# Last stage of a two-block model kernel turned from features to tokens in the partitions

## The chip, the cores and the metric

The kernel runs as one program on one core of a Trainium2 chip. The metric is the device time of that program in microseconds (us); before the change it is 944.46 us, the median of three runs (943.92 to 945.84). The engines that matter are TensorE (PE, with its weight loads as PEld), VectorE (DVE), ScalarE (ACT) and SyncE (SP), which only issues transfers here.

## The reference

A first block (short convolution mixer, convolutional feed-forward, latent attention, feed-forward) feeds a second one (a gated linear attention mixer and a squared-ReLU MLP). The change concerns only the end of the second block, for 256 tokens of 1024 features:

```python
h_lat = h_lat + mod_l[5] * sqrelu_mlp(modulate(rmsnorm(h_lat, norm2_g[i]), mod_l[3], mod_l[4]),
                                      mlp_w1[i], mlp_w2[i])
...
return rmsnorm(h_lat, final_g)
```

`sqrelu_mlp` is relu(x @ w1)**2 @ w2, with w1 of 1024 x 4096 and w2 of 4096 x 1024. The last matrix product, the gated addition to `h_lat` (1024 gates `mod_l[5]`, one per feature) and the last row norm with its gains `final_g` are what is rewritten. Everything is float32.

## The kernel before

**Weights as a stream.** All weights come through SP from DRAM in units of 128 x 1024 numbers (512 KB), into a ring of four tiles `raw`. Of each unit ACT makes a rounded copy `whi` (`hi`, L1007) and DVE the rest `wlo` = `raw` - `whi` (`lo`, L1528). Activations are kept in the same two parts. A product takes three matmuls: high by high, low by high, high by low. The rings `whi` and `wlo` have four slots too, so `hi` of unit u waits until PE is done with unit u - 4, and SP loads unit u when DVE has finished `lo` of unit u - 4. `slots_done` counts finished `lo`, `pe_units` counts units that PE has used up.

**The last stage** (`mlp_down`, 32 units) has the features of the output in the partitions. `units` multiplies with a 128 x 128 block of weights as the stationary operand and the 256 tokens as the moving one. In the first 28 units the high and the low part of the activations pass in one matmul of 512 columns (L501, `both=m2`), and a second one of 256 columns takes the low weights (L502). In the last 4 units there are three matmuls of 256 columns (L498, L499, L502). Four units make one tile of 128 output features; eight tiles go in turn to the PSUM banks `ps[0]` and `ps[1]`. DVE adds each tile with its gate to `h` (L2251), ACT squares it (L1016), DVE adds up the squares (L1546).

**The end.** After the last tile: DVE adds it to `h` (L2251), ACT squares it (L1500), PE sums the squares over the partitions (`column_stat`, L564 and L567), ACT takes the root (L1028), DVE the reciprocal (L1560), PE spreads it over the partitions (`spread`, L575), DVE multiplies `h` in four parts (L2270), and SP stores the four parts (L421). The gains were put on `h` by ACT meanwhile (`gained`, L1489).

**Other names.** `moving` (L530 to L532) is a function already in the kernel, used for the value projections and for some keys: there activations are the stationary operand and 512 columns of weights move. `h` holds the residual stream. `x2` (with its halves `xhi`, `xlo`), `yhi`, `ylo`, `khi`, `klo`, `zhi`, `zlo` and `m2` (with `mhi`, `mlo`) hold activations of different stages. `side` and the `ada` tiles carry the weights of the gates, whose dot products DVE makes between other work; the last of them belong to `mlp_up`, the stage ahead of the last. `vt` is a table of per-feature vectors, loaded at the start.

All on-chip tiles lie one behind the other in each partition, in the order of their declaration (`sb`), and tiles of stages that exclude each other share space. Worked out from the declared sizes, `x2` starts 95,136 bytes into the partition, `yhi` and `ohi` and `m2` at 111,520, `khi` at 177,056, `zhi` at 208,896 and `zlo` at 217,088; `whi` and `wlo` start at 16,384 and 32,768.

The order of the work is written out by hand: each engine's program is a list, with semaphores between them. Most stages are unrolled; the first 24 units of the last stage are a loop of three.

Of the kernel before, what the change touches and what calls it, by code (L numbers as in the profile page):

```python
# [23 lines left out]
P = 128  # L24
T = 256
# [20 lines left out]
OUT_PARTS = ((0, 2), (2, 4), (4, 6), (6, 8))  # L46
# [52 lines left out]
for _name, _n in [("g_mix0", 8), ("g_ffn0", 8), ("g_kvin", 8), ("g_mix1", 8), ("g_q", 4), ("g_kv", 2),  # L99
                  ("g_ffn1", 8), ("g_fin1", 8), ("g_n1", 8), ("g_n2", 8), ("g_fin2", 8), ("g_head", 8),  # L100
# [77 lines left out]
def program(nc, stream, xT, ctxT, vec, cst, rot, wa2, crow, out):  # L178
# [5 lines left out]
    with ctx:  # L184
# [105 lines left out]
        stage = ExitStack()  # L290
        m2 = sb("m2", 2 * MC * T, F32R, stage)
# [5 lines left out]
        raw_bias = sb("raw_bias", 4, F32, stage)  # L297
        stage.close()
# [63 lines left out]
        def _(sp):  # L362
# [52 lines left out]
            with sp.Fori(0, POSITIONS // RING - done // RING) as g:  # L415
                load_group(g * RING + done, g * RING + done - RING)
            for p in range(POSITIONS // RING * RING, POSITIONS):
                load_next(p)
            for n, (first, last) in enumerate(OUT_PARTS):
                sp.wait_ge(ev("out_chunk"), n + 1)  # L420
                sp.dma_start(out[:, first * T:last * T], h[:, first * T:last * T]).then_inc(ev("stored"), 16)  # L421
            sp.wait_ge(ev("stored"), 16 * len(OUT_PARTS))

# [12 lines left out]
        def _(pe):  # L436
# [537 lines left out]
            c.take(y_ready, MC - LATE)  # L974
            c.n["y_ready"] += LATE
            looped(DC // 2 - 1, 8, MC, mhi, mlo, lag=2, final=c.n["y_ready"], both=m2)
            units(4, MC, mhi, mlo, lag=2, both=m2)
            units(4, MC, mhi, mlo, lag=2)
            column_stat("last_square")
            spread()  # L980

        @block.scalar
        def _(act):
# [504 lines left out]
            def gained(k):  # L1488
                act.activation(at(h, k), at(h, k), ACT.Copy, scale=col("g_fin2", k)).then_inc(ev("gained"), 1)  # L1489

            def mlp_down(first, last=False):
                for m in range(2):
                    hi(4)
                    if last and m == 1:
                        act.wait_ge(sq_ready, c.value(sq_ready))
                        for k in range(DC - 1):
                            gained(k)
# [9 lines left out]
            with c.loop(DC // 2 - 1, {hi_ready: 8, tile_read: 2, sq_ready: 2}) as i:  # L1507
                mlp_down(i * 2)
# [764 lines left out]
def columns(v, n):  # L2273

    return v.reshape(n, P).T
# [107 lines left out]
```

## Time and profile before

| | us |
|---|---|
| median of 3 runs | 944.46 |
| lowest and highest | 943.92, 945.84 |
| profiled execution, first to last instruction (its span) | 944.4 |
| of it PE busy | 933.6 |
| first matmul of the last stage starts at | 847.01 |
| its last product matmul ends at | 936.09 |
| first store of the result is issued at | 939.71 |

The profile page gives an execution as its span; there is 0.1 us between that and the median of the runs, so nothing else of size lies around it. In the rows further down, times are from the start of the span, "x48" counts instructions, and a duration of a matmul overlaps with the next one: what a matmul costs in a stream is the distance between two starts, called its pitch here.

### The profile page before, as it was taken

Reading aid. Unit: us, or ns where it says so; the run is one execution under the profiler, and the core shown is the slowest. Engines: PE = TensorE matmul, PEld = TensorE weight load, DVE = VectorE, ACT = ScalarE, POOL = GpSimd, SP = SyncE. Lnnn points to the kernel's source line nnn. Section 1 sums busy time; section 2 is a strip of 40 time slices with the busy share of each in tenths; the row PEclk is TensorE's granted clock in tenths of the full one; section 3 lists DMA queues with packets and bytes.
Section 4 is the critical chain, followed back from the end, with each engine's and each line's share of the span. In section 5 each row is a group of like instructions: output and inputs, shape, how many; then the busy total and the mean of one; then the engine's idle time right before and its main releaser. Section 6 shows DMA issues by size and latency. Waiting matters only on the chain.

```text
span 944.4 us, 19749 instructions
## 1 busy us (share of the span) xinstructions
PE 933.6 (99%) x6952; PEld 889.8 (94%) x6952; DVE 798.0 (85%) x1317; ACT 564.0 (60%) x934; POOL 1.8 (0%) x8
## 2 busy tenths in 40 slices
PE   9999999999999999999999999999999999999997
PEld 8999999999999999999999999988899988888886
DVE  6999899999989888899999987955868889886553
ACT  6645656666455665766666556977533668674342
POOL 0000000000000000000000000000000000000000
PEclk9999999999999999999999999999999999999998
DMA  8776575557776554565557765563674348776661
GB/s 296 245 268 229 184 273 193 195 181 277 250 269 208 174 180 157 179 199 179 183 192 269 250 241 180 175 225 134 222 252 173 112 158 265 234 236 223 180 199 44
DMA packets 53877, 195.49 MB, mean 207 GB/s; under 512 B 6110, under 2 KB 6366, under 8 KB 53696
## 3 DMA queue, kind: packets, MB, share of 16 engines
q1 hardware_dynamic: 53680, 193.72, 61.5%
q10 hardware_dynamic: 144, 1.05, 0.3%
q8 instruction: 35, 0.57, 0.2%
q14 instruction: 18, 0.15, 0.0%
HBM read 193.69 MB, written 1.05 MB: 206 GB/s over the span
## 4 chain that ended last, share of the span: by engine, by line
PE 94%; DVE 4%; ACT 1%; issue 1%; DVEq 0%; ACTq 0%
PE ps L502 25%; PE ps L498 20%; PE ps L499 19%; PE ps L501 10%; PE ps L530 2%; PE ps L532 2%; PE ps L531 2%; DVE wlo L1528 1%; PE ps L609 1%; PE ps L792 1%; PE ps L808 1%; PE ps L651 1%; PE ps L652 1%; PE ps L653 1%; PE ps L674 1%
## 5 line engine op out<-in xcount | busy, mean ns | idle before, releaser
L1528 DVE TENSOR_TENSOR wlo<-raw,whi 128x1024 fp32r<-128x1024 f32 x303 | 367.0, 1220 | 72.9 <-ACT whi L1007 71.8
L1007 ACT ACTIVATE whi<-raw 128x1024 fp32r<-128x1024 f32 x303 | 317.0, 1052 | 90.8 <-PE ps L502 58.9
L502 PE MATMUL ps<-x,wlo 128*128 128x256 f32 x1248 | 349.5, 280 | 0.0
L498 PE MATMUL ps<-x,whi 128*128 128x256 f32 x1024 | 289.1, 282 | 0.0
L499 PE MATMUL ps<-x,whi 128*128 128x256 f32 x1024 | 286.9, 280 | 0.0
L502 PEld LDWEIGHTS ps<-x,wlo 128*128 128x128 f32 x1248 | 234.9, 188 | 0.0
L498 PEld LDWEIGHTS ps<-x,whi 128*128 128x128 f32 x1024 | 192.8, 188 | 0.8 <-issue 0.2
L499 PEld LDWEIGHTS ps<-x,whi 128*128 128x128 f32 x1024 | 192.8, 188 | 0.6 <-issue 0.5
L502 PE MATMUL ps<-yhi,wlo 128*128 128x256 f32 x400 | 112.1, 280 | 0.0
L498 PE MATMUL ps<-yhi,whi 128*128 128x256 f32 x400 | 112.1, 280 | 0.0
L499 PE MATMUL ps<-ylo,whi 128*128 128x256 f32 x400 | 112.1, 280 | 0.0
L1053 ACT ACTIVATE cv<-U,vt 128x256 f32<-128x256 f32 x88 | 44.9, 511 | 85.4 <-DVE U L1672 85.4
L501 PE MATMUL ps<-x,whi 128*128 128x512 f32 x224 | 78.1, 393 | 1.0 <-DVE mr L2212 0.6
L501 PE MATMUL ps<-m,whi 128*128 128x512 f32 x224 | 77.7, 392 | 0.0
L498 PEld LDWEIGHTS ps<-yhi,whi 128*128 128x128 f32 x400 | 75.3, 188 | 0.0
L499 PEld LDWEIGHTS ps<-ylo,whi 128*128 128x128 f32 x400 | 75.3, 188 | 0.0
L502 PEld LDWEIGHTS ps<-yhi,wlo 128*128 128x128 f32 x400 | 75.3, 188 | 0.0
L502 PE MATMUL ps<-m,wlo 128*128 128x256 f32 x256 | 71.6, 280 | 0.0
L501 PEld LDWEIGHTS ps<-x,whi 128*128 128x128 f32 x224 | 42.0, 188 | 11.0 <-DVE wlo L1528 1.0
L501 PEld LDWEIGHTS ps<-m,whi 128*128 128x128 f32 x224 | 42.1, 188 | 9.3
L502 PEld LDWEIGHTS ps<-m,wlo 128*128 128x128 f32 x256 | 48.0, 188 | 0.0
L1570 DVE SCALAR_TENSOR_TENSOR cv<-U,vt,cv 128x256 f32<-128x256 f32 x96 | 45.9, 479 | 0.6 <-ACT cv L1153 0.6
(333 smaller groups left out, 1536.6 us busy)
## 6 DMA issues: line engine op xcount, KB each, us to landing
raw<-stream SPq DMA_DIRECT2D x343, 512.0 KB, 4.0
side<-stream SPq DMA_DIRECT2D x16, 512.0 KB, 4.7
h<-xT SPq DMA_DIRECT2D x2, 512.0 KB, 6.1
c<-ctxT ACTq DMA_DIRECT2D x1, 1024.0 KB, 6.2
out<-h SPq DMA_DIRECT2D x4, 256.0 KB, 2.4
ct<-cst SPq DMA_DIRECT2D x1, 898.5 KB
rt_tab<-rot SPq DMA_DIRECT2D x1, 704.0 KB
state<-crow SPq DMA_DIRECT2D x1, 512.0 KB, 6.5
```

The source lines that it names most:

```text
L498: pe.matmul(dst, whi[:, w], at(hi, k), start=(k == 0), stop=False)
L499: pe.matmul(dst, whi[:, w], at(lo, k), start=False, stop=False)
L501: pe.matmul(ps[t % lag][:, :], whi[:, w], halves_of(both, k), start=(k == 0), stop=False)
L502: last = pe.matmul(dst, wlo[:, w], at(hi, k), start=False, stop=(k == K - 1))
L530: pe.matmul(dst, hi[:, tok], whi[:, w], start=first, stop=False)
L531: pe.matmul(dst, lo[:, tok], whi[:, w], start=False, stop=False)
L532: last = pe.matmul(dst, hi[:, tok], wlo[:, w], start=False, stop=final)
L609: pe.matmul(ps[7][:, 0:T], U[:, 0:P], U[:, 0:T], start=True, stop=True)
L1007: c.sig(act.activation(whi[:, s * D:(s + 1) * D], raw[:, r * D:(r + 1) * D], ACT.Copy), hi_ready)
L1053: c.sig(act.activation(at(cv, j), U[:, j * (T + 2) + 2:(j + 1) * (T + 2)], ACT.Copy, scale=vt_col(i * 12 + (base + 3 * j + 2))), tap_ready)
L1528: c.sig(dve.tensor_tensor(wlo[:, w], raw[:, r], whi[:, w], ALU.subtract), slots_done)
L1570: c.sig(dve.scalar_tensor_tensor(out=at(cv, j), in0=U[:, o + 1:o + T + 1], scalar=w1, in1=at(cv, j), op0=ALU.mult, op1=ALU.add), seq_dve)
```

## The change

The last stage is turned around. The output now has tokens in the partitions: `ps[2 * n + tk]` collects token half `tk` (128 tokens) of the features n * 512 to n * 512 + 511. The stationary operand is a 128 x 128 piece of the activations, the moving one is 512 columns of weights. The columns of w2 are laid out on the host as `wide`, in two halves of 16 units each.

- Matmuls: 12 of 512 columns per unit instead of 8 of 512 and 8 of 256 (the same 6144 columns). The last 4 units are taken first for token half 0, then for token half 1.
- The residual `h` has to be turned. DVE transposes it in 32 x 32 blocks (`turned_h`, eight instructions) behind `lo` of units 5 to 12, and SP moves the blocks to their place in `h_rows` with 32 transfers of 32 partitions x 8 x 32 numbers, eight each behind the loads of units 17 to 20.
- The gates are needed as a row in every partition: SP writes `mod[:, 5 * DC:6 * DC]` to DRAM (`gate_out`, 1024 single numbers) behind the load of unit 6 and reads it back into 128 partitions behind that of unit 8. The gains of the last norm come as a row from DRAM (`gain_row`, 512 KB) during `mlp_up`.
- Per quarter of the output (`row_sum`): DVE multiplies the bank with the gates, adds to `h_rows`, multiplies with the gains; ACT squares with an accumulated sum. Two quarters follow unit 19 and 20, two are at the end. The row norm needs no PE: root on ACT, reciprocal on DVE, and each quarter is scaled by one factor per partition, the first half of the features by ACT, the second by DVE. The result is stored as rows, in four parts.
- The column `g_fin2` leaves `vt`, which is 8 columns shorter; `m_pad` of 8 columns is put ahead of `m2`. With the declared sizes every tile behind `vt` starts 32 bytes earlier (`x2` at 95,104, `zhi` at 208,864), except `m2` and those behind it, which stay.

The core of the diff:

```diff
+        sb("m_pad", 8, F32, stage)
         m2 = sb("m2", 2 * MC * T, F32R, stage)
...
+            for p in range(done, POSITIONS):
                 load_next(p)
...
+                if u == GATE_AT:
+                    sp.wait_ge(ev("gate_known"), 1)
+                    sp.dma_start(gate_out.rearrange("k p -> p k"), mod[:, 5 * DC:6 * DC], allow_slow_non_contiguous=True)\
+                        .then_inc(ev("gate_stored"), 16)
...
+                elif ROWS_AT <= u < ROWS_AT + 4:
+                    if u == ROWS_AT:
+                        sp.wait_ge(ev("h_turned"), DC)
+                    for j in range(8):
+                        row_block(u - ROWS_AT, j)
...
-            looped(DC // 2 - 1, 8, MC, mhi, mlo, lag=2, final=c.n["y_ready"], both=m2)
-            units(4, MC, mhi, mlo, lag=2, both=m2)
-            units(4, MC, mhi, mlo, lag=2)
-            column_stat("last_square")
-            spread()
+            def row_products(slot, u, tk):
+
+                n, pair = u // HALF_UNITS, u % HALF_UNITS
+                for b in range(2):
+                    k = 2 * pair + b
+                    w = slice(slot * D + b * W, slot * D + (b + 1) * W)
+                    tok = slice(k * T + tk * P, k * T + (tk + 1) * P)
+                    dst = ps[2 * n + tk][:, :]
+                    pe.matmul(dst, mhi[:, tok], whi[:, w], start=(k == 0), stop=False)
+                    pe.matmul(dst, mhi[:, tok], wlo[:, w], start=False, stop=False)
+                    last = pe.matmul(dst, mlo[:, tok], whi[:, w], start=False, stop=(k == MC - 1))
+                return last
...
+            for u in range(MC - SPLIT, MC):
+                late.append(slot_of_next_unit())
+                last = row_products(late[-1], u, 0)
+            last.then_inc(ev("rows_done"), 1)
+            for u in range(MC - SPLIT, MC):
+                last = row_products(late[u - MC + SPLIT], u, 1)
+            last.then_inc(ev("rows_done"), 1)
...
+                new, old = row_part(gained, n, tk), row_part(h_rows, n, tk)
+                dve.tensor_tensor(new, ps[i][:, :], gate_row[:, n * W:(n + 1) * W], ALU.mult).then_inc(ev("row_gated"), 1)
+                dve.wait_ge(ev("row_gated"), i + 1)
+                dve.tensor_tensor(old, old, new, ALU.add).then_inc(ev("rows_summed"), 1)
+                dve.wait_ge(ev("rows_summed"), i + 1)
+                dve.tensor_tensor(new, old, gain_row[:, n * W:(n + 1) * W], ALU.mult).then_inc(ev("rows_gained"), 1)
...
+            while c.n["unit"] < UNITS:
+                lo()
+                u = c.n["unit"] - 1 - PHASE_AT["mlp_down"]
+                if 0 <= u - TURNS_AT < DC:
+                    turn_h(u - TURNS_AT)
+                elif u in (HALF_UNITS + RING - 1, HALF_UNITS + RING):
+                    row_sum(0, u - HALF_UNITS - RING + 1)
+                elif u == HALF_UNITS + RING + 4:
+                    row_bias()
```

The end of PE's program before, where the last tile's products are followed by the sums over the partitions and the spreading (the names after "<-" are moving and stationary operand):

```order
L502 MATMUL ps1<-m2,wlo 128x256
L564 MATMUL ps4<-ct,ssum 128x1 [waits ssum_ready,root_ready]
L564 MATMUL ps4<-ct,ssum 128x1
L567 MATMUL ps4<-ct,sq 128x1 [waits last_square]
L567 MATMUL ps4<-ct,sq 128x1
L575 MATMUL ps4<-ct,spare 128x128 [waits rstd_ready]
```

Nothing of this follows the products any more. The first products of the last stage now, behind those of `mlp_up` in `ps3`:

```order
L549 MATMUL ps3<-x2,wlo 128x256
L1031 MATMUL ps0<-whi,m2 128x512 [waits y_ready,tile_read,slots_done]
L1032 MATMUL ps0<-wlo,m2 128x512
L1033 MATMUL ps0<-whi,m2 128x512
```

Operands have changed places and every matmul has 512 columns. SP's list in the last stage now, with the issues that stand between the loads (before there were only loads and the four stores):

```order
L400 DMA raw<-stream 128x1024 [waits slots_done] x9
L447 DMA h_rows<-turned_h 32x8x32 [waits h_turned]
L447 DMA h_rows<-turned_h 32x8x32 x7
L400 DMA raw<-stream 128x1024 [waits slots_done]
L447 DMA h_rows<-turned_h 32x8x32 x8
L400 DMA raw<-stream 128x1024 [waits slots_done]
```

Each load of units 18 to 21 stands behind eight transfers of 32 partitions. DVE's list at its end now:

```order
L2343 TENSOR_TENSOR gained<-ps,gate_row 128x512 [waits rows_done]
L2345 TENSOR_TENSOR h_rows<-h_rows,gained 128x512 [waits row_gated]
L2347 TENSOR_TENSOR gained<-h_rows,gain_row 128x512 [waits rows_summed]
L2357 RECIPROCAL sums<-root 128x1 [waits row_root]
L2361 TENSOR_SCALAR gained<-gained,sums 128x512 [waits rows_gained,row_factor]
```

These five come once for each token half; the four multiplications of all of `h` (L2270) are gone.

## Rows read from the trace of the kernel before

**Rows 1.** The page: busy time of each engine, share of the span and instructions.

```profile
PE 933.6 (99%) x6952; PEld 889.8 (94%) x6952; DVE 798.0 (85%) x1317; ACT 564.0 (60%) x934; POOL 1.8 (0%) x8
```

**Rows 2.** Busy by stretch: the last stage, then the end behind it.

```profile
core 0: us, PE busy (x) PEld busy (x) DVE busy (x) ACT busy (x) POOL busy (x), PEclk, DMA share, GB/s
847.01:936.09 89.08, 89.08 (x549) 79.77 (x547) 48.79 (x58) 36.93 (x48) 0.00 (x0) 1.00 0.52 166
936.09:944.40 8.31, 1.66 (x13) 1.29 (x11) 3.13 (x6) 1.10 (x3) 0.00 (x0) 0.70 0.34 126
```

**Rows 3.** Who waited for whom in 847:936: total us, times, longest.

```profile
ACT whi L1007 <- PE ps L502: 23.2, 14, 1.7
DVE wlo L1528 <- ACT whi L1007: 22.4, 20, 1.5
```

**Rows 4.** Timeline of PE at the start of the last stage: start, us, instruction.

```profile
847.01 0.39 PE L501 MATMUL ps<-m,whi 128*128 128x512 f32 x1
847.24 0.28 PE L502 MATMUL ps<-m,wlo 128*128 128x256 f32 x1
847.36 0.39 PE L501 MATMUL ps<-m,whi 128*128 128x512 f32 x1
```

**Rows 5.** Busy by stretch where activations are stationary: x, z, then k.

```profile
629.66:640.86 11.20, 11.20 (x49) 9.01 (x48) 5.96 (x6) 10.97 (x14) 0.00 (x0) 1.00 0.51 162
666.08:668.80 2.72, 2.72 (x13) 2.25 (x12) 2.65 (x5) 2.04 (x3) 0.00 (x0) 1.00 0.59 193
317.06:318.46 1.40, 1.40 (x8) 1.13 (x7) 1.36 (x3) 1.06 (x1) 0.00 (x0) 1.00 0.83 225
```

**Rows 6.** Busy by stretch, 256 moving columns: x, x again, z.

```profile
105.00:220.00 115.00, 115.00 (x983) 115.00 (x982) 110.78 (x204) 74.24 (x124) 0.00 (x0) 1.00 0.62 212
392.00:510.00 118.00, 118.00 (x997) 118.00 (x996) 113.45 (x208) 75.58 (x127) 0.00 (x0) 1.00 0.58 194
742.00:756.00 14.00, 14.00 (x119) 13.99 (x118) 13.31 (x24) 11.09 (x19) 0.00 (x0) 1.00 0.60 195
```

**Rows 7.** Timeline of the end.

```profile
936.13 0.48 DVE L2251 SCALAR_TENSOR_TENSOR h<-ps,mod,h 128x256 f32<-128x256 f32 x1 [7.60 <-PE ps L502]
936.65 0.42 ACT L1500 ACTIVATE sq<-h 128x256 f32<-128x256 f32 x1 [6.58 <-DVE h L2251]
937.12 0.61 PE L567 MATMUL ps<-ct,sq 128*128 128x1 f32 x4 [0.69 <-ACT sq L1500]
937.82 0.17 ACT L1028 ACTIVATE root<-ps 128x2 f32<-128x2 f32 x1 [0.21 <-PE ps L567]
938.02 0.17 DVE L1560 RECIPROCAL spare<-root 128x2 f32<-128x2 f32 x1 [1.41 <-ACT root L1028]
938.24 0.71 PE L575 MATMUL ps<-ct,spare 128*128 128x128 f32 x4 [0.52 <-DVE spare L1560]
938.99 2.48 DVE L2270 TENSOR_TENSOR h<-h,ps 128x512 f32<-128x512 f32 x4 [0.80 <-PE ps L575]
```

**Rows 8.** Stores of the result: durations of the issues, then issue to landing.

```profile
L421 SPq DMA_DIRECT2D out<-h x4: 332/338/344, 939.7 to 941.5; - x4
DMA to landing us min/median/max: 2.3/2.4/2.5
```

**Rows 9.** Durations of 128x512 work on DVE and ACT, and of ACT's accumulator read.

```profile
L2052 DVE TENSOR_TENSOR qf<-E,ee x4: 684/685/686, 662.7 to 671.1; 128x512 f32<-128x512 f32 x4
L1426 ACT ACTIVATE osq<-ps x4: 597/598/601, 709.1 to 730.4; 128x512 f32<-128x512 f32 x4
L1217 ACT ACTIVATION_READ_ACCUMULATOR sm<-ps,mx x16: 192/198/211, 338.1 to 363.2; 128x1 f32 x16
```

**Rows 10.** Timeline of the last stage: `hi` and `lo` of one unit, one `hi` later.

```profile
897.13 1.06 ACT L1007 ACTIVATE whi<-raw 128x1024 fp32r<-128x1024 f32 x1 [1.62 <-PE ps L502]
898.23 1.23 DVE L1528 TENSOR_TENSOR wlo<-raw,whi 128x1024 fp32r<-128x1024 f32 x1 [1.27 <-ACT whi L1007]
908.22 1.06 ACT L1007 ACTIVATE whi<-raw 128x1024 fp32r<-128x1024 f32 x1 [1.71 <-PE ps L502]
```

**Rows 11.** Timeline of SP at the start; transfers of 850:920; issues with landing.

```profile
1.66 0.90 SPq L369 DMA_DIRECT2D raw<-stream  x2
...
q1 hardware_dynamic: 3827, 13.97, 63.3%
...
raw<-stream SPq DMA_DIRECT2D x26, 512.0 KB, 4.2
```

**Rows 12.** Transfers of 0:2.6, nearly all small packets.

```profile
DMA packets 158, 0.06 MB, mean 24 GB/s; under 512 B 144, under 2 KB 144, under 8 KB 158
...
q1 hardware_dynamic: 158, 0.06, 11.1%
```

More of the change, by code:

```diff
@@ L297, in program @@
         raw_bias = sb("raw_bias", 4, F32, stage)
+        stage.close()
+        stage = ExitStack()
+        sb("inner_held", 8 + 2 * MC * T + 8 * T, F32, stage)
+        turned_h = sb("turned_h", DC * T, F32, stage)
+        gained = sb("gained", 2 * D, F32, stage)
+        sb("raw_held", 24, F32, stage)
+        h_rows = sb("h_rows", 2 * D, F32, stage)
+        gate_row = sb("gate_row", D, F32, stage)
+        gain_row = sb("gain_row", D, F32, stage)
+        sums = sb("sums", 8, F32, stage)
         stage.close()
@@ L414, in _, with loads_to @@
                 load_down(first, done)
-            with sp.Fori(0, POSITIONS // RING - done // RING) as g:
-                load_group(g * RING + done, g * RING + done - RING)
-            for p in range(POSITIONS // RING * RING, POSITIONS):
-                load_next(p)
[L419 to L422, printed above, removed]
+            def loads_to(last, done):
+                with sp.Fori(0, (last - done) // RING) as g:
+                    load_group(g * RING + done, g * RING + done - RING)
+                return last
@@ L1486, in _ @@
             inner_hi(MC - 1)
[L1488 to L1497, printed above, removed]
-                        c.take(tile_read)
-                        act.wait_ge(ssum_ready, c.value(sq_ready, -1))
-                        act.activation(at(sq, 1), at(h, DC - 1), ACT.Square).then_inc(ev("last_square"), 1)
-                        act.wait_ge(ev("last_square"), 1)
-                        gained(DC - 1)
-                    else:
-                        c.take(tile_read)
-                        square(h, first + m, m)
@@ L2261, in _ @@
[L2261 to L2270 removed]
+            dve.memset(sums[:, :], 0.0).then_inc(ev("gate_known"), 1)
@@ new lines, in _ @@
+            while c.n["unit"] < UNITS:
[7 more added lines that the diff above has]
+                    row_bias()
+            for tk in range(2):
+                row_sum(1, tk)
+                row_scaled(tk)
@@ L2324, in lay_out @@
         tiles(gla["r"]),
-        tiles(a["gla_w_o_2"][0]), tiles(a["mlp_w1_2"][0]), tiles(a["mlp_w2_2"][0]),
+        tiles(a["gla_w_o_2"][0]), tiles(a["mlp_w1_2"][0]), wide(a["mlp_w2_2"][0]),
     ]
```

135 lines of the change are left out of this document (94 added, 41 removed).

## Prediction

> **What bounds the kernel now.** I read the page first, then the last stage by stretches, then the waits there, then the end instruction by instruction. PE is busy 933.6 of 944.4 us [rows 1]. In the last stage it is busy for all of 89.08 us, from the first product at 847.01 to the end of the last at 936.09, at the full granted clock (1.00) [rows 2]. ACT waits for PE there (23.2 us in 14 waits), DVE for ACT (22.4 us), and PE is in no row as the one that waits [rows 3]. So inside the stage only PE's own pitch counts; behind it 8.31 us follow that nothing hides [rows 2]. The change acts on both, and a third thing moves with it: where tiles lie.
>
> **The last stage on PE.** Before, a pair of 512 and 256 columns takes 847.36 - 847.01 = 0.35 us [rows 4]; the stage as a whole, 28 units of 8 pairs and 4 units of 24 matmuls of 256, takes 89.08 us, which is 2.78 per unit. After, 32 x 12 = 384 matmuls of 512 columns with activations as the stationary operand. The trace has this form, and with two prices: with x stationary 48 matmuls in 11.20 us, 0.2333 each, with k 6 in 1.40, 0.2333, with z 12 in 2.72, 0.2267 (each count in the row includes one or two that were already running) [rows 5]. 384 pitches give 89.60 or 87.05 us; the last matmul outlives its pitch by 0.16 us (0.39 long [rows 4]), so the stage would take 89.8 or 87.2 us: **+0.7 or -1.9 us**.
>
> What separates x and k from z? Not the clock (1.00 in all three), and not how busy DVE and ACT are: k and z lie beside a DVE that is nearly full and x beside one half idle. What I find is the address: the starts of `x2` and `khi` leave 32 when divided by 64, that of `zhi` leaves 0. `m2` leaves 32 before and after. So I take the price of x and k, +0.7, and keep -1.9 as the other end.
>
> The Trainium skill, page "TensorE: Matmul & The Clock Gate", section "Back-to-back issue gap", gives columns / 2.4 GHz + 2.5 ns for a matmul in a stream. By that rule the 512 columns would take 215.8 ns, and the saving would be the 160 matmuls fewer (544 before, 384 after) times 2.5 ns, or 0.4 us. The rows are 11 to 18 ns above it and show two prices for one shape, so the trace does not agree.
>
> **Addresses elsewhere.** With `vt` 32 bytes shorter, x and k leave 0 and z leaves 32. By the same reading 96 matmuls with x stationary and 24 with k become 0.0067 us cheaper each (-0.8), 144 with z dearer (+1.0): **+0.2 us**. What the shift does to the far larger number with x or y as the moving operand is a rival below; I take zero, since neither end is certain.
>
> **The end.** Before: add 0.48, square 0.42, PE sums 0.61, root 0.17, reciprocal 0.17, spread 0.71, four multiplications 2.48, with handovers 936.09 to 941.47 [rows 7]; the last store is issued at 941.5, lands 2.4 us later [rows 8] at 943.9, and 0.5 more passes to the end. After, for token half 1, on the path: gating from PSUM 0.68 and adding 0.69 on DVE [rows 7, 9], ACT's square 0.60 and the read of its accumulator 0.20 [rows 9], root and reciprocal 0.17 each [rows 7], scaling on ACT 0.60. That is 3.1, and with six handovers of 0.04 some 3.35 us. The gain multiplication (0.69) lies beside the square, DVE's scaling beside ACT's. Two stores are left, issued 0.45 apart [rows 11]; the second lands 2.4 later, and 0.5 to the end: 3.35 + 0.45 + 2.4 + 0.5 = 6.7 us instead of 8.3, **-1.6 us**. Unknown is how long a DVE multiplication by a per-partition factor takes, 0.35 to 0.69, and the handovers: -1.2 to -2.1. Token half 0 has 24 matmuls of cover, 5.6 us, for its own chain of about 3.5, so it is ready when half 1 ends; a cover under that would put up to its DVE work, some 2.7 us, on the path.
>
> **Work that I cost at nothing.** DVE has 2.8 us per unit and uses 1.23 for `lo`. Eight transposes of 128 x 256, whose kind no row shows, may take from 0.4 to 1.5 us each and still fit. `row_sum` is 2.1 us behind `lo` of units 19 and 20, so `lo` of unit 20 is late by about a microsecond. The cover: `hi` starts at 897.13 and `lo` ends at 899.46, 2.3 us after PE freed the slot, and PE comes to it after three units, 8.4 us: 6 us to spare [rows 10]. ACT's two squares (0.8 each) fit as well. `gain_row` and `gate_row` are 512 KB each, which is 1.7 us of transfer at the rate of the stretch (13.97 MB in 63.3% of 70 us is 315 GB/s) [rows 11]. The loads have 908.22 - 899.5 - 4.2 = 4.5 us to spare [rows 10, 11], and the rest of the cover behind that.
>
> **The transfers of h** need their own count, since SP issues them ahead of loads, and `lo` of unit 20 stands on DVE behind `row_sum`, which waits for all 32. SP takes 0.45 per issue [rows 11], so a batch of eight and a load take 4.05 us where a unit takes 2.8. On the 16 transfer engines a batch is 2048 pieces of 128 bytes, 128 per engine. In the first 2.6 us there are 158 packets in 11.1% of 16 engines, 4.6 us; 14 large ones at 0.185 (70 us x 16 x 63.3% / 3827) leave 2.0 us for 144, 0.014 each [rows 11, 12]. So 1.8 us for the batch and 1.7 for the load: less than SP needs. At the other end, with the price of a large packet, it would be 24 us. Let zero be the moment at which PE frees the slot of unit 13. The first batch starts at 2.3, four take 16.2, landing 2.4: 20.9. DVE wants them at 19.1 and waits 1.8. PE needs `lo` of unit 20 at 28.0, and `row_sum` with `lo` takes 3.3: the limit is 24.7. So nothing reaches PE as long as a batch with its load stays under 5.0 us, **0 us**; it is a cover of 4 us, not a wide one.
>
> **Sum.** +0.7 +0.2 -1.6 = -0.7 us on a span of 944.4, which is 0.1 below the median: **943.7 us**. A measurement of this kernel can tell about 0.2%, 1.9 us, from no change, so this is "within 0.2%" (942.6 to 946.3).
>
> **Rivals.**
> 1. **The low pitch.** The difference in rows 5 has a cause other than the address, and m comes out like z. For it: one correlation over three tiles is thin. Against it: x and z lie close together (11.2 us at 630, 2.7 us at 666) and each holds its price. Stage -1.9, elsewhere 0, end -1.6: 941.0, faster.
> 2. **The batches reach PE (slower).** SP's issue grows with the pieces of a transfer: 256 of them here, 128 in every row I have. From 0.55 us per issue on, the limit of 5.0 is passed, and PE waits four times the excess: at 0.65 (a batch and load of 5.65) 2.6 us, at 0.90 (7.65) 10.6 us. The same holds if pieces cost over 26 ns on the engines. For it: nothing in the trace has this shape, and the cover is small. Against it: SP's issues last 332 to 344 ns whatever they carry [rows 8]. 946 to 954.
> 3. **The shift by 32 bytes costs where activations move (slower).** With 256 moving columns x has 115.0 / 981 = 0.1172 and later 118.0 / 995 = 0.1186, z has 14.0 / 117 = 0.1197 [rows 6]. If z is dearer because it leaves 0, then x, y, o and k become so too: about 2500 matmuls by 2.5 ns and 1800 by 1.1 ns, 8.2 us in all. Against it: x itself has both 0.1172 and 0.1186 at one address, so something else moves this pitch as much. 945.5 to 952. The opposite sign, a gain of 2 to 4 us (940 to 942), cannot be excluded either.
> 4. **It doesn't do what it says**: PE waits at the start of the stage or between the halves for something that I have missed. 944 to 947.
>
> **How the numbers follow.** Main case 0.40, rival 1 0.20, rival 2 0.16, rival 3 0.14 and its opposite 0.06, rival 4 0.04. The main case has 0.08 of its 0.40 below 942.6 and 0.03 above 946.3; rival 1 has 0.17 below. Faster by over 0.2%: 0.08 + 0.17 + 0.05 = 0.30. Slower: 0.03 + 0.15 + 0.13 + 0.01 = 0.32. Within: 0.38. The range reaches down over rival 1 with the largest gain at the end, and up over the smaller half of rivals 2 and 3: 940.5 to 951.0. The main case alone would span 942.4 to 945.0.
>
> **What would show it.** In the changed profile: 12 matmuls of the last stage in 2.80 us (rival 1: 2.72); z stationary at 0.2333 and x stationary at 0.2267, the plainest test of the address; 256 moving columns with x in the first third at 0.1172 or at 0.120 (rival 3); SP's issues of `h_rows` in batches under 4 us, and no idle time of PE around units 18 to 23 (rival 2: PE waits for `lo` of unit 20 or DVE for `h_rows` for long); 6.7 us from the last product to the end. The prediction fails if any stage ahead of the last moves by more than 1 us, or if PE is idle in the last one.

## The result: 1.6% slower, and the profile after

| | before | after |
|---|---|---|
| median of 5 runs | 945.84 | 960.56 |
| lowest and highest | 943.92, 947.93 | 957.97, 961.61 |
| span of the profiled execution | 944.4 | 959.6 |
| first product of the last stage starts at | 847.01 | 855.80 |
| its last product ends at | 936.09 | 953.04 |
| from there to the end | 8.31 | 6.56 |

The ratio is 1.0156 (95% interval 1.0137 to 1.0175). The forecast was 943.7 us with a range up to 951.0, so the time lies outside it. The three markers divide the 15.2 us by which the spans differ into **+8.79** ahead of the last stage, **+8.16** in it and **-1.75** behind it. The time of an execution lies 1.8 us above its own span (961.42 us for the profiled one of 959.6), not 0.1: the small gap of the kernel before came from comparing a median with the span of another execution. One of the seven executions of the last kernel in experiment 6 took 1138.40 us at a mean granted clock of 0.753; no ratio here uses it, and without it the median there would be 938.19 instead of 939.30.

The last stage and the end by stretches, as in [rows 2] (busy us and count of each engine, granted clock, share of the transfer engines, GB/s):

```profile
855.80:953.04 97.24, 92.71 (x386) 73.60 (x384) 48.05 (x57) 35.14 (x42) 0.00 (x0) 0.96 0.64 173
953.04:959.60 6.56, 0.00 (x0) 0.00 (x0) 2.73 (x5) 1.74 (x4) 0.00 (x0) 0.74 0.23 88
```

PE was busy for the whole of the stage before; now 4.5 us are missing, and the granted clock is no longer 1.00. The waits of that time (854 to 960 us), to be read beside [rows 3], say for whom:

```profile
ACT whi L1079 <- DMA raw<-stream: 22.5, 12, 6.1
ACT mr L1563 <- DVE h_rows L2345: 14.6, 4, 5.9
DVE gained L2343 <- DMA h_rows<-turned_h: 6.8, 1, 6.8
...
PE ps L1031 <- DVE wlo L1605: 4.5, 2, 4.0
```

ACT waits for weights that haven't arrived, DVE for the turned `h`, and PE, which was in no such row before, for `lo`. The order of DVE's list ties the last two together. `row_sum` waits 6.8 us for the transfers of `h`, and the `lo` for which PE stands comes behind it:

```profile
913.43 0.69 DVE L2343 TENSOR_TENSOR gained<-ps,gate_row 128x512 f32<-128x512 f32 x1 [6.78 <-DMA h_rows<-turned_h]
...
915.49 1.22 DVE L1605 TENSOR_TENSOR wlo<-raw,whi 128x1024 fp32r<-128x1024 f32 x1
```

What PE does behind its longest wait is in its timeline:

```profile
916.76 0.80 PE L1031 MATMUL ps<-whi,m 128*128 128x512 f32 x1 [3.97 <-DVE wlo L1605]
917.35 0.63 PE L1032 MATMUL ps<-wlo,m 128*128 128x512 f32 x1
917.78 0.63 PE L1033 MATMUL ps<-whi,m 128*128 128x512 f32 x1
918.21 0.63 PE L1031 MATMUL ps<-whi,m 128*128 128x512 f32 x1
```

Starts are 0.43 us apart where they should be 0.233: 512 columns in 0.427 us is the 1.2 GHz level of the clock. It lasts to 922.0: one pitch of 0.59 and eleven of 0.43, 2.5 us more than at 2.4 GHz. So the stage is +0.7 for the pitch (0.2333, as forecast), 4.5 for two waits (0.6 and 4.0), 2.5 for the clock behind the longer one, and some 0.4 more. Counted from start to start the same two places hold all of it: 0.8 us over the pitch around the first wait (at 881 us) and 6.7 around the second add up to 7.5, and 0.7 + 7.5 is the 8.16.

Ahead of the last stage PE stands for 4.1 us in all, before and after (842.86 us busy of 847.01, and 851.66 of 855.80). So only its pitch differs, with 256 moving columns (the stretches of [rows 6], x, x again and z, a little later; this is after):

```profile
106.00:220.00 114.00, 114.00 (x952) 114.00 (x951) 108.50 (x198) 72.47 (x121) 0.00 (x0) 1.00 0.61 207
397.00:510.00 113.00, 113.00 (x944) 113.00 (x943) 107.49 (x198) 71.46 (x120) 0.00 (x0) 1.00 0.55 182
749.00:763.00 14.00, 14.00 (x120) 13.96 (x119) 13.04 (x24) 11.32 (x20) 0.00 (x0) 1.00 0.57 188
```

The kernel before has 974 and 955 matmuls in the first two of these. Not a line of PE's program for these stages changed.

Last, SP, on which the rest will turn. Its timeline has the gate's write, a stand of 9.8 us until that write has landed (the read of `gate_row` waits for it), and then the batches of eight transfers of `h` between the loads:

```profile
859.88 0.39 SPq L454 DMA_DIRECT2D gate_out<-mod  x1
861.00 1.46 SPq L400 DMA_DIRECT2D raw<-stream  x2
872.30 0.33 SPq L458 DMA_DIRECT2D gate_row<-gate_out  x1
...
888.18 5.61 SPq L447 DMA_DIRECT2D h_rows<-turned_h  x8
893.83 0.60 SPq L400 DMA_DIRECT2D raw<-stream  x1
894.48 5.81 SPq L447 DMA_DIRECT2D h_rows<-turned_h  x8
```

### The profile page after: what moved, and what is told of

Same layout as the page of the kernel before. It is cut to its first block, busy times and chain, and to the rows that moved or that the text cites. A ratio compares the mean times of both kernels' runs of the same rounds, so it can differ in the third digit from the quotient of the medians.

```text
span 959.6 us, 19208 instructions
## 1 busy us (share of the span) xinstructions
PE 944.4 (98%) x6780; PEld 890.4 (93%) x6780; DVE 797.9 (83%) x1315; ACT 562.7 (59%) x929; POOL 1.8 (0%) x8
## 4 chain that ended last, share of the span: by engine, by line
PE 86%; DVE 6%; DMA 3%; SPq 2%; ACT 2%; issue 1%; ACTq 0%; DVEq 0%
PE ps L549 21%; PE ps L546 19%; PE ps L545 19%; PE ps L548 5%; DVE wlo L1605 2%; PE ps L577 2%; PE ps L578 2%; PE ps L579 2%; SPq L447 2%; DMA raw<-stream 1%; PE ps L1031 1%; DMA gate_out<-mod 1%; PE ps L1033 1%; PE ps L1032 1%; PE ps L656 1%
## 5 line engine op out<-in xcount | busy, mean ns | idle before, releaser
L549 PE MATMUL ps<-x,wlo 128*128 128x256 f32 x1248 | 354.3, 284 | 0.0
L1031 PE MATMUL ps<-whi,m 128*128 128x512 f32 x128 | 52.2, 408 | 4.5 <-DVE wlo L1605 4.5
L1033 PE MATMUL ps<-whi,m 128*128 128x512 f32 x128 | 51.4, 402 | 0.0
L1032 PE MATMUL ps<-wlo,m 128*128 128x512 f32 x128 | 51.2, 400 | 0.0
L1647 DVE SCALAR_TENSOR_TENSOR cv<-U,vt,cv 128x256 f32<-128x256 f32 x96 | 45.8, 477 | 0.6 <-ACT cv L1225 0.6
L1653 DVE SCALAR_TENSOR_TENSOR cv<-U,vt,cv 128x256 f32<-128x256 f32 x96 | 45.7, 476 | 0.1
```

What stands on the lines that cost most here:

```text
L549: last = pe.matmul(dst, wlo[:, w], at(hi, k), start=False, stop=(k == K - 1))
L1031: pe.matmul(dst, mhi[:, tok], whi[:, w], start=(k == 0), stop=False)
L1032: pe.matmul(dst, mhi[:, tok], wlo[:, w], start=False, stop=False)
L1033: last = pe.matmul(dst, mlo[:, tok], whi[:, w], start=False, stop=(k == MC - 1))
L1647: c.sig(dve.scalar_tensor_tensor(out=at(cv, j), in0=U[:, o + 1:o + T + 1], scalar=w1, in1=at(cv, j), op0=ALU.mult, op1=ALU.add), seq_dve)
L1653: return dve.scalar_tensor_tensor(out=at(cv, j), in0=U[:, o:o + T], scalar=w0, in1=at(cv, j), op0=ALU.mult, op1=ALU.add)
```

## The experiments

**The way of reading.** Three causes were suspected: where the tiles lie, the batches of `h` transfers, and the gate's write. Medians are compared with those of the kernel before on the same chips, which lay between 944.9 and 945.9 us; the ratio and its interval say more than the difference of two medians.

### 1. The kernel before with moved tiles

```
         vt = sb("vt", NVEC)
+        sb("shift", 8)
...
+        sb("m_pad", 8, F32, stage)
         m2 = sb("m2", 2 * MC * T, F32R, stage)
```

> The kernel before, with one edit: 8 unused columns (32 bytes) behind the table vt and 8 more ahead of m2. Every address has the remainder by 64 that it has in the changed kernel (x2, yhi, khi 0; zhi 32; m2 32), no instruction differs. Theory A (the addresses slow the stages ahead of the last): the first product of the last stage comes at 855.8 instead of 847.0, the time is 8.8 us above that of before, 953 to 954; x moving takes 0.1184 to 0.1200 instead of 0.1172 to 0.1184, z stationary 0.2333 instead of 0.2267, x stationary about 0.2327 or less. Theory B (something else of the change, the split loops of SP, the gain row's load or the code's length, slows them): the time is that of before within 1 us.

Measured: 931.74 us, ratio 0.9863 (0.9829 to 0.9898). The sign was wrong. 64 bytes of unused space make the kernel 1.4% faster, and the reading of the prediction, that the rest of a start divided by 64 decides, is refuted: `x2` leaves 0 both here and in the changed kernel, and is cheap here and dear there. The place does matter, by more than any term of my sum.

### 2. The changed kernel with the places of before

```
+        sb("shift", 8)
...
-        sb("m_pad", 8, F32, stage)
         m2 = sb("m2", 2 * MC * T, F32R, stage)
```

> The changed kernel with one edit: 8 unused columns behind vt and none ahead of m2, so that all tiles have the remainders by 64 of the kernel before (x2, yhi, khi, m2 32; zhi 0). Theory A: the 8.8 us ahead of the last stage are gone, the time is 960.6 - 8.8 = 951.8, and PE still stands idle for some 4 us before unit 20 with a lowered clock after it. Theory B: it stays at 960.

Measured: 953.13 us, ratio 1.0071 (1.0048 to 1.0095). As expected: the stages ahead of the last are back (first product of the last at 845.12), and what is left is in the last stage. Half of the loss (7.4 of 14.7 us) is the shift of 32 bytes.

### 3. The transfers of h spread

Four transfers behind each of eight loads instead of eight behind each of four. Two things more move with it: the first two row sums and ACT's squares of them come six units later, and the gate is read back behind the load of unit 12 instead of 8:

```
-                elif u == GATE_AT + 2:
+                elif u == GATE_AT + 6:
...
-                elif ROWS_AT <= u < ROWS_AT + 4:
+                elif ROWS_AT <= u < ROWS_AT + 8:
...
-                    for j in range(8):
-                        row_block(u - ROWS_AT, j)
+                    for j in range(4):
+                        row_block((u - ROWS_AT) // 2, (u - ROWS_AT) % 2 * 4 + j)
...
-                elif u in (HALF_UNITS + RING - 1, HALF_UNITS + RING):
-                    row_sum(0, u - HALF_UNITS - RING + 1)
+                elif u in (HALF_UNITS + RING + 5, HALF_UNITS + RING + 6):
+                    row_sum(0, u - HALF_UNITS - RING - 5)
```

In the first run at the places of the change, in the second at those of before:

> The changed kernel with SP's extra issues spread: four transfers of h behind each of eight loads (units 17 to 24) instead of eight behind each of four, the first two row sums behind units 25 and 26 instead of 19 and 20, and the gate row read back behind the load of unit 12 instead of 8. Addresses as in the changed kernel. Theory of the batches: SP's 0.66 us per issue makes a batch with its load 5.9 us, over the 5.0 that PE bears; spread out, it is 3.2 us against 2.8 per unit, the lateness stays under 4 us, and PE's idle time in the last stage (4.7 us) and the low clock after it (2.3 us) go: 960.6 - 7.2 = 953.4. If the idle time comes from the number of small pieces on the transfer engines, it stays in part: 956 to 960.

> Both edits at once: the addresses of the kernel before and SP's issues spread. If the two causes are all there is and do not interact, the time is 960.6 - 8.8 - 7.2 = 944.6 by the runs of the changed kernel, and counted from the kernel before +0.7 for the pitch of the stage, -1.75 at the end: 944.5 - 1.0 = 943.5. If there is a third cause, it stays above 946.

Measured: 956.22 us, ratio 1.0120 (1.0086 to 1.0154), and 948.59 us, ratio 1.0020 (1.0000 to 1.0040). The three edits together take 4.3 and 4.5 us off. The first time lies in the range that its expectation gave to a rival (956 to 960: the small pieces of `h` on the transfer engines). Its profile speaks against that rival: PE's longest wait there is 1.1 us at 875.8, before the first transfer of `h`. Whether the spread or the later row sums removed the long wait, no run separates: in the changed kernel `whi` of that unit was finished at 911.1 and PE ran out of work at 912.8, so a `lo` of 1.2 us with no row sum ahead of it would have come in time there, by my estimate from these rows, even with the batches as they were.

The second time is above 946, so by its own expectation a third cause is at work. Its waits name it:

```profile
ACT whi L1079 <- DMA raw<-stream: 15.1, 7, 9.6
...
PE ps L1031 <- DVE wlo L1605: 3.4, 1, 3.4
```

The 9.6 us fall at 868 us, before the first transfer of `h`. What SP issued ahead of these loads is the gate's write; the list of transfers in 845:948 gives its size and the time to its landing, where a load of 512 KB needs 4 to 5 us:

```profile
gate_out<-mod SPq DMA_DIRECT2D x1, 4.0 KB, 15.2
```

### 4. The gate turned before it is written

DVE transposes the 32 columns of `mod` around the gate, and four transfers of 8 pieces of 128 bytes replace one of 1024 pieces of 4 bytes:

```
+            dve.transpose(turned_gate[:, :], mod[:, 4 * DC:8 * DC]).then_inc(ev("gate_known"), 1)
...
-                    sp.dma_start(gate_out.rearrange("k p -> p k"), mod[:, 5 * DC:6 * DC], ...)
+                    for i in range(4):
+                        sp.dma_start(gate_out[:, 32 * i:32 * (i + 1)],
+                                     turned_gate[32 * i + DC:32 * i + 2 * DC, :])
```

First together with the spread, then alone, both at the places of before:

> The changed kernel with the addresses of before and the spread transfers, as the run just before it (948.6 us), and one edit more: VectorE transposes the columns of the modulation that hold the gate, and the gate row leaves in four transfers of 8 pieces of 128 bytes, where one transfer of 1024 pieces of 4 bytes stood. Theory A, the 1024 small writes hold up the weight loads issued behind them: ScalarE's wait of 9.6 us for the raw weights at 868 us goes, with it TensorE's idle 3.4 us at 870 and the matmuls at a low clock after it (about 1.3 us): 943.9 us, the end still 6.6 us, no idle piece of TensorE over .3 us in the last stage. Theory B, the loads are late for another reason (the h transfers beside them): the wait and 948.6 us stay.

> The changed kernel with the addresses of before, its h transfers in batches of 8 as the change has them, and the gate row turned by VectorE and written in 128-byte pieces. It stands between the run with neither edit (953.1 us) and the one with both (944.0), beside the one with the spread transfers alone (948.6). Theory A, the two waits are separate and add: the batches alone cost what is left of 9.1 us after the gate's 4.6, so 948.5 us, and TensorE idles 3 to 4 us after one of the batches. Theory B, the batches (5.2 to 5.8 us each) only hurt because the loads are already late from the small writes: 944 to 945.5 us, and no idle over .5 us.

Measured: 943.99 us, ratio 0.9996 (0.9980 to 1.0012), and 951.55 us, ratio 1.0053 (1.0030 to 1.0076). The first meets its expectation of 943.9: the wait of 9.6 us is gone, and so is every wait of PE in the last stage. At the places of before, the change without its waits is level with the kernel before. What the small pieces do is seen on the transfer engines, in the same 13 us behind the gate's write, first with them (the second run of experiment 3), then without:

```profile
853.00:866.00 13.00, 13.00 (x57) 10.45 (x57) 3.70 (x5) 2.12 (x2) 0.00 (x0) 1.00 0.99 101
```

```profile
853.00:866.00 13.00, 13.00 (x58) 10.45 (x57) 7.70 (x10) 4.53 (x5) 0.00 (x0) 1.00 0.78 268
```

Busy for 0.99 of the time they move 101 GB/s, and 268 GB/s at 0.78 without the small pieces. Where the gate is read back two loads later, as in the change, SP adds a stand of its own (9.8 us there, 11.2 in experiment 2) in which it issues no load:

```profile
SPq L458 <- DMA gate_out<-mod: 9.8, 1, 9.8
```

The last stage alone, in the four kernels at one and the same place (neither edit, spread, gate, both):

```profile
845.12:945.29 100.17, 92.77 (x386) 73.37 (x384) 48.00 (x57) 35.17 (x42) 0.00 (x0) 0.97 0.63 168
```

```profile
847.23:942.17 94.94, 91.56 (x386) 73.00 (x384) 48.33 (x57) 35.34 (x42) 0.00 (x0) 0.98 0.68 177
```

```profile
847.50:943.52 96.02, 92.65 (x386) 73.78 (x384) 48.68 (x58) 35.13 (x42) 0.00 (x0) 0.96 0.57 175
```

```profile
845.86:935.62 89.76, 89.75 (x386) 71.90 (x384) 48.74 (x58) 35.24 (x42) 0.00 (x0) 1.00 0.60 188
```

The stage without waits takes 89.76 us, and the forecast for it was 89.8. The gate's write alone adds 5.2 (with the gate read back behind unit 12), the batches alone 6.3, both 10.4. So theory A of the last expectation holds in kind (two waits that nearly add) and theory B falls. Its 948.5 us was missed. Part of that lies ahead of the stage, which begins at 845.12, 847.23, 847.50 and 845.86 in these four profiles though PE's program is the same up to there; and the batches cost more than the difference I took them from. That spread of 2.4 us is also why the times show only 1.6 us between the first and the third of these kernels, where the stage shows 4.2. SP's timeline in that run shows the batches as slow as ever with the small writes gone:

```profile
878.79 5.32 SPq L448 DMA_DIRECT2D h_rows<-turned_h  x8
884.15 0.60 SPq L401 DMA_DIRECT2D raw<-stream  x1
884.80 5.75 SPq L448 DMA_DIRECT2D h_rows<-turned_h  x8
```

Batch and load are 5.9 and 6.4 us here, 24.1 us for all four, against the limit of 5.0 each that the prediction worked out. In the run with both edits a batch of four takes 2.70 and the load behind it 0.60, 3.3 us, and nothing waits.

### 5. What it is about the place

Three shifts of the kernel before, with nothing else changed. One moves the weights' halves and the activations together, two move the activations alone:

```
         raw = sb("raw", RING * D)
+        sb("shift", 8)
```

> The kernel before with 8 unused columns (32 bytes) ahead of the halves of the weights and nothing else: weights and activations both start 32 bytes later, so the distance between the two stays what it is before (160 modulo 256), while the activations lie where the run of 931.7 us had them (192). Theory A, what counts is the start of the activations by itself: moving windows of 256 columns at .1134 us a matmul in the stretches of x, and 931.7 us. Theory B, what counts is how weights and activations lie to each other: .1174 and .1186 us as before, and 945.9 us. Theory C, the start of each operand counts by itself, the weights' too: neither of the two.

```
         vt = sb("vt", NVEC)
+        sb("shift", 16)
```

> The kernel before with 16 unused columns (64 bytes) behind the vectors: x, y, k and m start at 224 modulo 256, z at 64, the weights' halves where they were. Over 256 moving columns the starts seen so far cost, beyond the columns' own 106.7 ns: 12.9 to 14.2 ns at 0, 10.3 to 12.0 at 32, 12.0 to 13.5 at 128, 10.7 to 12.2 at 160, 6.8 at 192, 11.6 at 224. Theory A, this goes by the start modulo 128 (0 dearest, 64 cheapest, 32 and 96 between): z at 64 moves at 6.8 ns where it has 13.3 before, x stays at about 11.6, and the whole is at or under 945.9 us, about 943. Theory B, it goes modulo 256 and only 192 is cheap: z at 64 keeps 11 to 13 ns, and the whole is 945 to 948.

The third has 24 in place of 16:

> The kernel before with 24 unused columns (96 bytes) behind the vectors: x, y, k and m start at distance 0 modulo 256 from the weights' halves, z at 96. If the distance modulo 256 sets the pitch, x with 256 moving columns takes what z took at 0, 13.3 ns over 106.7 (z of before), where x has 10.4 to 12.1 before: about 4,000 matmuls by 1.5 to 2.5 ns, +6 to +10 us, 952 to 956 us, the slowest place of all. The stretch with both operands of 512 and 256 columns and m at 0 is the unknown. If what the runs at 160 and 192 showed is the place of single tiles instead, no rise is due: 944 to 948 us.

Measured: 945.38 us, ratio 1.0004 (0.9987 to 1.0021); 950.82, ratio 1.0051 (1.0033 to 1.0069); 958.65, ratio 1.0126 (1.0099 to 1.0153). The first is the decisive one, and its theory B holds. `x2` starts exactly where the run of 931.74 us had it, and the time and the pitch are those of the kernel before: this address by itself does nothing. What counts is how far the activations start behind the weights' halves. In the table, "distance" is the start of the activations less the start of `whi`, divided by 256, the rest of it. The same 114 us of x with 256 moving columns, in the order of the table:

```profile
106.00:220.00 114.00, 114.00 (x974) 114.00 (x973) 109.78 (x204) 73.43 (x123) 0.00 (x0) 1.00 0.63 212
```

```profile
106.00:220.00 114.00, 114.00 (x974) 114.00 (x973) 110.52 (x204) 73.70 (x123) 0.00 (x0) 1.00 0.64 213
```

```profile
106.00:220.00 114.00, 114.00 (x1008) 114.00 (x1007) 112.13 (x213) 76.31 (x129) 0.00 (x0) 1.00 0.67 226
```

```profile
106.00:220.00 114.00, 114.00 (x966) 114.00 (x965) 109.61 (x202) 72.85 (x123) 0.00 (x0) 1.00 0.62 208
```

```profile
106.00:220.00 114.00, 114.00 (x952) 114.00 (x952) 107.53 (x198) 71.86 (x121) 0.00 (x0) 1.00 0.61 204
```

| kernel | distance of x | matmuls in 114 us | pitch, ns | median, us |
|---|---|---|---|---|
| before | 160 | 974 | 117.3 | 945.84 |
| both moved (32 bytes ahead of the ring) | 160 | 974 | 117.3 | 945.38 |
| experiment 1 | 192 | 1008 | 113.3 | 931.74 |
| 64 bytes behind `vt` | 224 | 966 | 118.3 | 950.82 |
| 96 bytes behind `vt` | 0 | 952 | 120.0 | 958.65 |
| after (its rows are above) | 128 | 952 | 120.0 | 960.56 |

The pitch is 114 us by the count less 2, since a count includes those running at its ends. Of the theories for the second, A (64 a cheap distance like 192, for z) was wrong: z at 64 moves at 106.7 + 11.2 ns, not + 6.8. B was right in kind, but the time is 3 us above its 945 to 948. Over the columns' own 106.7 ns the profiles show 12 to 14 ns at distances 0, 96 and 128, 10 to 12 at 32, 64, 160 and 224, and 6.7 at 192 alone. A rule with half the period is unlikely: z has 13.8 ns at 96 and 12.1 at 224, and 11.2 at 64 where x has 6.7 at 192, though no tile was seen at both 64 and 192. The third kernel behaves as forecast for x, but is slower than its 952 to 956. Its last stage starts 10.9 us later than before (857.86), where 6 to 10 were expected, and the stage of m itself, with its matmuls of 512 and 256 columns in turn, takes 1.5 us longer: 397 matmuls in 70 us, where the kernel before has 405.

### 6. The place of the activations in the changed kernel

The kernel with both edits of experiment 4, `x2` and all behind it 32 bytes further (distance 192, z at 32), then with `m2` at distance 0:

> The kernel of the gate transpose (expected 943.9 us) with x, y, k and m starting at 192 modulo 256 and z at 32, where the run of 931.7 us had the first three. Theory A, the gains add: the stages ahead of the last at the pitches of that run (x moving .1134 us), the first product of the last stage 14 us or so earlier than at 160, the last stage at .229 to .2333 us a matmul, the end 6.6: 929 to 931 us, below both kernels. Theory B, a faster stage ahead of the last makes the weight loads late in the last one (the transfers are read more often): idle of TensorE there again, 933 to 937 us.

```
+        sb("m_pad", 16, F32, stage)
         m2 = sb("m2", 2 * MC * T, F32R, stage)
```

> The kernel of 928.7 us with m, and u in its place, 64 bytes later: m starts 0 modulo 256 behind the weights' halves, where it starts 192. Stationary activations with 512 moving columns showed 13.3 ns over the columns' 213.3 at distance 0 (z of before), 15.5 at 192 (m of this kernel), 20.0 at 160. Theory A, the distance sets it whichever tile stands there: 13.3 ns in the last stage, 384 matmuls by 2.2 ns less, -.8 us, and 927.9 us. Theory B, 0 was good for z alone: 15 to 20 ns, 928.5 to 930.5 us.

Measured: 928.74 us, ratio 0.9818 (0.9797 to 0.9839), and 927.09 us, ratio 0.9803 (0.9783 to 0.9823). The gains add, as theory A had it. In the last stage, 70 to 77 us of it without a wait at distance 160, 192 and 0:

```profile
849.60:920.00 70.40, 70.40 (x303) 56.67 (x302) 38.71 (x45) 28.46 (x30) 0.00 (x0) 1.00 0.71 223
```

```profile
838.00:910.00 72.00, 72.00 (x316) 59.06 (x316) 39.65 (x42) 29.26 (x31) 0.00 (x0) 1.00 0.69 211
```

```profile
837.00:914.00 77.00, 77.00 (x341) 63.75 (x341) 42.40 (x47) 30.81 (x32) 0.00 (x0) 1.00 0.65 203
```

From start to start that is 0.2333, 0.2289 and 0.2267 us a matmul: m takes the price that z had before (0.2267, [rows 5]) once it lies at z's distance. The distance isn't all: x stationary at 0, in the kernel with 24 columns, takes 0.2288. The medians of these two kernels come from different chips and their intervals overlap, so that the second is the faster one rests on this row and not on the times. Both beat the kernel before by clear intervals. The last one lies below experiment 1 as well (0.9783 to 0.9823 against 0.9829 to 0.9898), by some 5 us. Not all of that is the change. In experiment 1 m lies at 224, and its last stage takes 90.65 us where the kernel before, with m at 160, takes 89.08; the old stage with m at a good place was not run. With m at 160 in both, stage and end together are 97.39 us before and 96.34 in the kernel of experiment 4 with both edits: 1 us for the change, near the 0.9 forecast for the two terms (+0.7 and -1.6).

Last, the changed kernel as it was made, batches and small writes left in, with only its tiles at 192:

```
+        sb("shift", 16)
...
-        sb("m_pad", 8, F32, stage)
         m2 = sb("m2", 2 * MC * T, F32R, stage)
```

> The changed kernel, its batches of 8 and its one small-piece transfer of the gate left as they are, with x, y, k and m 64 bytes on, at 192 modulo 256 behind the weights' halves. The same kernel at 160 was 953.1 us; the kernel before gained 14.2 us from 160 to 192. Theory A, the place is a cost by itself: 953.1 less 14 less 384 matmuls of the last stage by 4.4 ns (1.7), 937.4 us, and the change as written then measures faster than the kernel before, by 8 us, with its waits of 5 to 8 us in the last stage still there. Theory B, a faster stage ahead makes the waits for the loads longer: 939 to 943 us.

Measured: 939.30 us, ratio 0.9923 (0.9894 to 0.9952). It waits in the last stage as much as before (96.40 us from 829.79, and 5.4 us of PE's waits), and still it is faster than the kernel before. The sign of the verdict on this change hung on 64 bytes. That compares a well placed kernel with a badly placed one: beside experiment 1, where the kernel before has its x at 192 as well, it is some 7 us slower (931.74), though the two intervals just touch. Its theories, 937.4 and 939 to 943, lie too close together for this kernel's executions (most of them 934.57 to 940.60) to decide between them.

## Why the prediction failed, point by point

- **Addresses elsewhere, +0.2 us, with zero for x and y as the moving operand.** This is the first of the two steps that failed. The term was mis-sized: it measured +8.8 (847.01 to 855.80), of which the profile with the places restored gives all back. Rival 3 had the price right, 8.2 us, and got 0.14; as its rule is wrong, that the price fits is in part luck. I held against it that x has two pitches at one address, which was true but no reason: a second cause beside the place doesn't exclude the place. Its mechanism, the rest by 64, was wrong, and with it the reason for the opposite sign.
- **The address by its rest after division by 64 (x and k leave 32, z leaves 0).** Right that it is the place, wrong in the measure. The distance to the weights' halves is 160 for x, k and m and 0 for z; two of the three tiles seen at 0 as stationary operand pay 0.2267 (z of before, m of the kernel of 927.09 us). The announced test came out half: z stationary rose to 0.2333 as said, x didn't fall to 0.2267 (90 starts average 0.2324), as it now lies at distance 128. The sentence of the prediction that the trace doesn't agree with the rule for the gap holds: no place here came down to 215.8 ns for 512 columns.
- **The last stage on PE, +0.7.** Right: 0.2333 a matmul, 89.76 us for the stage once nothing waits. The value was the right one because m stays at 160 in the change; that the rest by 64 picked it was luck.
- **The end, -1.6 (6.7 us instead of 8.3).** Right: 6.56. The terms were off by little (square 0.63, root 0.29, ACT's scaling 0.72, DVE's 0.49) in both directions.
- **The transfers of h, 0 us, as long as a batch with its load stays under 5.0.** This is the second step that failed: PE loses 7.5 us in the stage to waits and what follows them. The limit was fair, the value was not. I priced SP's issue at 0.45 and put a higher one into rival 2 with 0.16; a batch takes 0.65 to 0.73 an issue, and the load behind it 0.60. The trace of before held a warning that I passed over. Its first plain loads, issued one behind the other, take up to 0.65:

```profile
L369 SPq DMA_DIRECT2D raw<-stream x4: 424/486/653, 1.7 to 4.5; - x4
```

  So SP's issues don't last 332 to 344 ns "whatever they carry". The chain itself was foreseen: DVE waits for the last transfer, with `lo` of unit 20 behind it, 6.8 us where I had 1.8. The rival's rule of four excesses gives 4 x (6.0 - 5.0) = 4.1 for the run with the batches alone; measured are 3.4 of idle time and 2.7 for the clock behind it, which the rule lacked. Its reason, the number of pieces, isn't shown, as the last section says.
- **The gate's write was in no term.** I counted the bytes of `gate_row` and not the 1024 pieces of `gate_out`, though the change says "single numbers". 4 KB took 12.4 to 15.2 us to land, the loads issued behind it came late, and PE lost 5.2 us where it acts alone. In the changed kernel itself its direct share is small, the wait of 0.6 us at 881. It is the step that the prediction should have bounded by pieces, as it did for `h`.
- **An idle PE was priced at its idle time.** After 3.4 to 5.5 us without work, in five profiles, the next 6 to 12 matmuls run at 0.43 us: 1.6 to 2.7 us on top, 2.5 in the changed kernel. Waits of 1.1 us and less were not followed by that.

By its own list of signs the prediction fails "if any stage ahead of the last moves by more than 1 us, or if PE is idle in the last one". Both happened, and each would have been enough.

## What to carry to other kernels

A change that makes one table shorter moves every tile behind it: work out, for the operands of the matmuls that fill the kernel, how far stationary and moving tile start apart modulo 256 bytes, before and after, and try a few pads of 32 bytes before judging any other edit; here they were worth 14 us of 945, more than the edit itself. Compare two versions each at its own best place. Count a transfer by its pieces on the transfer engines, and turn a column into pieces of 128 bytes before writing it to DRAM. Take the price of an issue from the densest run of issues in the trace, not from a lone one. Price a wait of the bounding engine of a few microseconds with the slow clock behind it.

## What the hardware did that was not expected

- **A pitch that goes by the distance of two tiles.** With weights stationary and 256 columns of activations moving, a matmul costs 106.7 ns for the columns and 6.7 (distance 192) to 13.8 ns (96) more; with activations stationary and 512 columns of weights moving it costs 213.3 ns and 13.3 (z and m at 0), 15 to 16 (192, and x at 0), 19 (128) or 20 ns (32, 160, 224) more. The order of places isn't the same in the two forms. The Trainium skill, page "TensorE: Matmul & The Clock Gate", section "Back-to-back issue gap", gives columns / 2.4 GHz + 2.5 ns, which it calls the gap of an isolated matmul, and about 131 ns for 512 columns in a stream with weight loads. The nearest that any place here came is 4.2 ns above the first, no row comes near the second, and the page has no word on places.
- **At one place the pitch can still change within a kernel.** In the kernel of 927.09 us y moves over the same tiles by the same lines on both sides of 247 us, and the clock is granted in full:

```profile
222.00:246.00 24.00, 24.00 (x214) 24.00 (x214) 22.96 (x35) 13.60 (x18) 0.00 (x0) 1.00 0.79 280
249.00:277.00 28.00, 28.00 (x239) 28.00 (x239) 24.75 (x37) 14.27 (x19) 0.00 (x0) 1.00 0.75 262
```

  That is 113.2 and 118.1 ns. Between the two PE has two slower starts (at 248.8 and 249.0 us); the profile of experiment 1 has such a spot too, and its pitch stays. The last kernel of experiment 6 shows it in the last stage, with m at 192 on both sides of PE's wait of 4.5 us at 890.8:

```profile
860.00:884.00 24.00, 24.00 (x107) 19.69 (x106) 9.09 (x9) 7.04 (x7) 0.00 (x0) 1.00 0.69 179
895.00:919.00 24.00, 24.00 (x104) 19.46 (x103) 11.10 (x11) 8.49 (x8) 0.00 (x0) 1.00 0.46 152
```

  From start to start that is 0.2289 and 0.2333. x of [rows 6], 0.1172 and 0.1186, may be the same. So the distance sets the pitch only in part; what switches it stays open, and is worth up to 5 ns a matmul. It may be one reason why four kernels with x at 192 come to the first product of the last stage at 829.79, 829.91, 832.55 and 833.16, though the third of them keeps its pitch at 247 us.
- **The price of an issue on SP isn't fixed, and doesn't go by the pieces alone.** A load of the stream takes 0.33 us in the middle, but 0.60 behind a batch. The transfers of `h`, 256 pieces each, take 0.61, while the gate's write with its 1024 pieces takes 0.39:

```profile
L447 SPq DMA_DIRECT2D h_rows<-turned_h x32: 586/610/1263, 888.2 to 911.4; - x32
L454 SPq DMA_DIRECT2D gate_out<-mod x1: 388/388/388, 859.9 to 859.9; - x1
```

  What the dear ones share is that they stand close behind other issues, as the first loads of the kernel before do. That this is the cause was not tested.
- **Small writes to DRAM hold up what is queued behind them.** Experiment 4 has the rows: 101 GB/s with transfer engines busy for 0.99 of the time. The Trainium skill, page "DMA: Bandwidth & Descriptors", section "Specifications", asks for 512 bytes or more a transfer for the full rate and says that below it the engines read, modify and write. That a 4 KB write in 1024 pieces takes 12.4 to 15.2 us agrees with it as far as it goes. Pieces of 128 bytes, also under 512, cost nothing that can be seen in the last versions; but with the size the number fell too, from 1024 to 32, and no run says which of the two decides.
